# Reordering the prologues of three norms, folding squares on VectorE in the first stage, and padding two small tables

## The reference, cut to what matters

```
def rmsnorm(x, w):
    xf = x.astype(jnp.float32)
    y = xf * lax.rsqrt(jnp.mean(xf * xf, axis=-1, keepdims=True) + EPS)
    return (y * w.astype(jnp.float32)).astype(x.dtype)
def modulate(h, shift, scale):
    return h * (1 + scale) + shift
...
        h = modulate(rmsnorm(x, norm1_w[l]), sh1, sc1)
        hc = modulate(rmsnorm(ctx, norm1_w[l]), csh1, csc1)
        ...
        x = x + g2 * peer(modulate(rmsnorm(x, norm2_w[l]), sh2, sc2), w_pq[l], ...)
    return rmsnorm(x, final_norm_w)
...
def layer_ab(x, norm_g, w_in, ...):
    h = rms_norm(x, norm_g)
...
def layer_c(x, norm_g, w_in, ...):
    h = rms_norm(x, norm_g)
    u, gate = jnp.split(h @ w_in, 2, axis=-1)
```

## Time and profile before

| | |
|---|---|
| median of 3 runs (lowest, highest) | 3998.22 us (3995.88, 3999.73) |
| the profiled execution, its own time | 4002.12 us |
| its span in the trace, mean granted clock | 4000.3 us, 0.91 |
| PE busy | 3238.5 us, 81% |
| DVE busy | 2427.1 us, 61% |
| ACT busy | 1187.9 us, 30% |
| POOL busy | 929.5 us, 23% |
| HBM read | 938.51 MB |

### The profile page before, as it was taken

The page is one execution under the profiler, slowest core; times in us unless marked ns, Lnnn a source line. Parts: engine busy times, 40 slices in busy tenths (PEclk is TensorE's granted clock), DMA queues, the critical chain, the costliest instruction groups (busy, mean ns, idle before and its releaser), DMA issues. The chain is left out here.

```text
span 4000.3 us, 39602 instructions
## 1 busy us (share of the span) xinstructions
PE 3238.5 (81%) x14024; PEld 2234.9 (56%) x14024; DVE 2427.1 (61%) x3283; ACT 1187.9 (30%) x1887; POOL 929.5 (23%) x791
## 2 busy tenths in 40 slices
PE   5899998759998928777777877777998778987598
PEld 1588776538797813223322323335886667876587
DVE  1556554658776485566556655546555457869575
ACT  1432122335434401111111111103454244644553
POOL 0000010010000056544554554530001116400010
PEclk8899998869998969999999999998999579998699
DMA  9567322019864479999999999994663034530064
GB/s 355 183 213 285 122 90 85 2 47 360 313 200 147 139 298 422 422 422 422 422 422 422 422 422 422 422 422 132 185 190 116 4 117 145 173 94 4 20 192 146
DMA packets 177323, 941.98 MB, mean 235 GB/s; under 512 B 21528, under 2 KB 26776, under 8 KB 99000
## 3 DMA queue, kind: packets, MB, share of 16 engines
q0 software_dynamic: 82944, 604.02, 36.8%
q1 hardware_dynamic: 94272, 336.67, 25.5%
HBM read 938.51 MB, written 2.10 MB: 235 GB/s over the span
## 5 line engine op out<-in xcount | busy, mean ns | idle before, releaser
L1616 PE MATMUL bank<-pe_v_rows,pe_diag 128*128 128x512 f32 x1920 | 907.3, 621 | 354.5 <-DMA pe_v_rows<-in_expert_v,pe_staged_v 211.6
L1479 DVE SCALAR_TENSOR_TENSOR pe_junk<-pe_u_rows,h_rows 128x2048 f32<-128x2048 f32 x256 | 587.0, 2293 | 459.4 <-DMA pe_u_rows<-in_expert_u,pe_staged_u 448.3
L1616 PEld LDWEIGHTS bank<-pe_v_rows,pe_diag 128*128 128x128 f32 x1920 | 362.2, 197 | 899.0 <-issue 483.6
L1424 POOL DMA_INDIRECT pe_v_rows<-in_expert_v,pe_staged_v x248 | 307.9, 1242 | 359.9 <-PE bank L1616 304.6
L1424 POOL DMA_INDIRECT pe_u_rows<-in_expert_u,pe_staged_u x256 | 335.7, 1311 | 228.3 <-DVE pe_junk L1479 134.4
L1577 ACT ACTIVATE pe_diag<-ident,pe_weights 128x128 f32<-128x128 f32 x240 | 91.6, 399 | 747.5 <-PE bank L1616 747.3
L268 PE MATMUL bank<-h_parts,b_top 128*128 128x512 f32 x768 | 271.3, 399 | 9.2 <-DVE b_rest L369 9.2
L369 DVE TENSOR_TENSOR in_rest<-in_ring,in_top 128x1024 fp32r<-128x1024 f32 x112 | 138.3, 1236 | 221.1 <-ACT in_top L338 221.0
L369 DVE TENSOR_TENSOR c_rest<-c_ring,c_top 128x1024 fp32r<-128x1024 f32 x128 | 176.4, 1385 | 100.5 <-ACT c_top L338 100.2
L369 DVE TENSOR_TENSOR ab_rest<-ab_ring,ab_top 128x1024 fp32r<-128x1024 f32 x112 | 136.9, 1225 | 148.7 <-ACT ab_top L338 148.6
L270 PE MATMUL bank<-h_parts,b_rest 128*128 128x256 f32 x768 | 215.3, 280 | 0.0
(11 more groups left out here) (541 smaller groups left out, 6442.9 us busy)
## 6 DMA issues: line engine op xcount, KB each, us to landing
b_ring<-in_w_mix SPq DMA_DIRECT2D x128, 512.0 KB, 6.3
in_ring<-in_w_in SPq DMA_DIRECT2D x112, 512.0 KB, 3.7
ab_ring<-in_w_ab SPq DMA_DIRECT2D x112, 512.0 KB, 3.8
mod_ring<-in_w_mod SPq DMA_DIRECT2D x32, 1024.0 KB, 8.1
v_rows<-in_w_mod POOLq DMA_DIRECT2D x32, 1024.0 KB, 5.4
k_cols<-in_w_mod POOLq DMA_DIRECT2D x32, 1024.0 KB, 8.3
c_ring<-in_w_c_in SPq DMA_DIRECT2D x64, 512.0 KB, 4.5
c_ring<-in_w_glu_out SPq DMA_DIRECT2D x64, 512.0 KB, 4.3
```

The costliest lines, as they stand in the source:

```text
L1424: gp.indirect_dma_start(buf[:, slot, :], None, table, bass.IndirectOffsetOnAxis(ap=staged[which][:, tile, e:e + 1], axis=0)).then_inc(sems ...
L1479: nc.vector.scalar_tensor_tensor(out=junk[:, :], in0=ub[:, s, :], scalar=1.0, in1=h2tm[:, tile, :], op0=ALU.mult, op1=ALU.mult, accum_out= ...
L1616: mm = nc.tensor.matmul(banks[4 * tile + b][:, :], diag[:, e % 4, :], vb[:, s, b * 512:(b + 1) * 512], start=False, stop=False, skip_group ...
```

## The change

1. In `SplitFirst.act_start` ScalarE casts the second weight half of a norm's stream behind the first quarter of the activations, not ahead of it.
2. In `SplitFirst.dve_start` VectorE scales a quarter ahead. With a shift (`pq`) the scaling of quarter `q + 1` stands ahead of the remainder of quarter `q`; without one (`ab`, `c`) only quarters 2 and 3 are scaled together ahead of the remainders 2 and 3.
3. In `stream` TensorE's part of the norm (`hooks.pe_start`) stands ahead of its wait for the small transfers (`small_in`). Only `ab` has both.
4. In the first stage VectorE adds the 16 tiles of squares into one (five instructions), and TensorE sums that one tile with one matmul behind unit 16.
5. `gains` and `modc` are allocated with 512 bytes per partition; what is read and written in them stays the same.

```diff
--- before.py
+++ after.py
@@ -179,20 +179,36 @@
         if self.norm:
             self.norm.act_root(act)
             cast()
-            cast()
         for q in range(4):
             if self.norm:
                 self.norm.act_shift(act, q)
             self.operand.cast(act, q)
+            if self.norm and q == 0:
+                cast()
 
     def dve_start(self, dve, subtract):
         if self.norm:
+            scale, remainder = self.norm.dve_scale, self.operand.subtract
             self.norm.dve_root(dve)
-            for q in range(4):
-                self.norm.dve_scale(dve, q)
-                if q < 2:
-                    subtract()
-                self.operand.subtract(dve, q)
+            scale(dve, 0)
+            if self.norm.shift is not None:
+                scale(dve, 1)
+                subtract()
+                remainder(dve, 0)
+                scale(dve, 2)
+                subtract()
+                remainder(dve, 1)
+                scale(dve, 3)
+            else:
+                subtract()
+                remainder(dve, 0)
+                scale(dve, 1)
+                subtract()
+                remainder(dve, 1)
+                scale(dve, 2)
+                scale(dve, 3)
+            remainder(dve, 2)
+            remainder(dve, 3)
             return
         for q in range(3):
             self.operand.subtract(dve, q)
@@ -236,9 +252,9 @@
 
         @block.tensor
         def _(pe):
+            hooks.pe_start(pe)
             if small:
                 pe.wait_ge(small_in, 16 * len(small))
-            hooks.pe_start(pe)
             before = None
             for seg in segments:
                 u0, ready, free = seg["at"], seg.get("ready"), seg["free"]
@@ -417,7 +433,7 @@
         small_in, x_in = sem("mod_small_in"), sem("mod_x_in")
         unit_in = [sem(f"mod_unit_in{s}") for s in range(RING)]
         units_used, wide_zeroed = sem("mod_units_used"), sem("mod_wide_zeroed")
-        squared, summed = sem("mod_squared"), sem("mod_summed")
+        squared, summed, folded = sem("mod_squared"), sem("mod_summed"), sem("mod_folded")
         silu_done, rows_done, turned = sem("mod_silu_done"), sem("mod_rows_done"), sem("mod_turned")
         mean_done, root_done, chain = sem("mod_mean_done"), sem("mod_root_done"), sem("mod_chain")
 
@@ -467,12 +483,9 @@
                     mm = nc.tensor.matmul(banks[g][32 * b:32 * b + 32, :], c_wide[:, k, :], ring[:, u % RING, b * 512:(b + 1) * 512],
                                           start=(k == 0), stop=(k == KT - 1))
                 mm.then_inc(units_used, 1)
-                if 8 <= u < 12:
-                    pe.wait_ge(squared, u - 7)
-                    for j in range(4 * (u - 8), 4 * (u - 8) + 4):
-                        mm = nc.tensor.matmul(banks[4][:, :], con["ones"], squares[:, j, :], start=(j == 0), stop=(j == KT - 1))
-                    if u == 11:
-                        mm.then_inc(summed, 1)
+                if u == 16:
+                    pe.wait_ge(folded, 1)
+                    nc.tensor.matmul(banks[4][:, :], con["ones"], squares[:, 0, :], start=True, stop=True).then_inc(summed, 1)
 
             for g in range(2):
                 pe.wait_ge(rows_done, g + 1)
@@ -495,6 +508,11 @@
             nc.vector.tensor_copy(fast(wg_parts[0][:, :, :]), wg[:, :, :]).then_inc(split_done, 1)
             dve.wait_ge(split_done, 1)
             nc.vector.tensor_tensor(fast(wg_parts[1][:, :, :]), wg[:, :, :], wg_parts[0][:, :, :], ALU.subtract).then_inc(split_done, 1)
+            for q in range(1, 4):
+                dve.wait_ge(squared, q + 1)
+                link(nc.vector.tensor_tensor(squares[:, 0:4, :], squares[:, 0:4, :], squares[:, 4 * q:4 * q + 4, :], ALU.add))
+            link(nc.vector.tensor_tensor(squares[:, 0:2, :], squares[:, 0:2, :], squares[:, 2:4, :], ALU.add))
+            nc.vector.tensor_tensor(squares[:, 0, :], squares[:, 0, :], squares[:, 1, :], ALU.add).then_inc(folded, 1)
             dve.wait_ge(summed, 1)
             nc.vector.tensor_scalar(rstd[:, :], banks[4][:, :], 1.0 / D, EPS, ALU.mult, ALU.add).then_inc(mean_done, 1)
             dve.wait_ge(root_done, 1)
@@ -2733,7 +2751,7 @@
 def consts(nc, st, ctx, t):
     ident = ctx.enter_context(nc.sbuf_tensor("ident", [P, P], F32))
     ones = ctx.enter_context(nc.sbuf_tensor("ones", [P, P], F32))
-    gains = ctx.enter_context(nc.sbuf_tensor("gains", [P, 6, KT], F32))
+    gains = ctx.enter_context(nc.sbuf_tensor("gains", [P, 8, KT], F32))
     with st.stage() as (block, sem):
         const_in = sem("const_in")
 
@@ -2741,7 +2759,7 @@
         def _(sp):
             sp.dma_start(ident[:, :], t["c_ident"]).then_inc(const_in, 16)
             sp.dma_start(ones[:, :], t["c_ones"]).then_inc(const_in, 16)
-            sp.dma_start(gains[:, :, :], t["gains"]).then_inc(const_in, 16)
+            sp.dma_start(gains[:, 0:6, :], t["gains"]).then_inc(const_in, 16)
             sp.wait_ge(const_in, 48)
     return {"ident": ident[:, :], "ones": ones[:, :], "gains": gains}
 
@@ -2846,7 +2864,7 @@
         att = ExitStack()
         with ExitStack() as s1:
             hT = sb("hT", [P, KT, 512], s1)
-            modc = sb("modc", [P, 32, 2], s1)
+            modc = sb("modc", [P, 64, 2], s1)[:, 0:32, :]
             ring = sb("mod_ring", [P, 4, UNIT], s1)
 
             first_gates_and_modulation(st, nc, t, hT, h, ring, banks, modc, c_silu, gate_rows, con)
```

## The result

The change runs in 3953.23 us (median of 4 runs, 3943.43 to 3957.92) where the kernel before runs in 3998.97 (4 runs, 3995.88 to 4001.78). The ratio is 0.9881, 95% interval 0.9861 to 0.9901: 45.7 us less, where I had forecast 22.6 less and a range that ended at 3966. The profiled execution took 3952.45 us (4002.12 before).

The account below looks back on a forecast made before the run. Each stage has its own bound: TensorE in the streams, DMA in the expert layer, `mod_ring` in the first stage, engine handoffs in prologues. Gains 6.1 + 8.7 + 2.6 + 2.1 + 3.1 = 22.6 us gave a median of 3975.6, range 3966 to 3985.

Parts of the forecast that it names:

- the two tables: Padding `gains` and `modc` shifts every buffer behind them: costed at 0, with 34 us either way in the expert layer as bounds.
- the right rival: Aligned rows speed the gathers in the DMA-bound expert layer: up to 34 us more gained, 3942 us; chance 7%.
- the two bounds: Expert layer: 34 us faster or slower from the buffers' new starts, 2.6% of 1298 us; left outside the range.
- First stage: Square sums folded on VectorE: unit 16 no longer waits, unit 31 comes 6.1 us earlier; range 4.7 to 7.5.
- The 1.4 us around unit 24: First stage: a further 1.4 us lost with no square sums beside it, assumed to stay.
- Prologue of `pq`: Scaling a quarter ahead and the later weight cast start TensorE's last piece 8.7 us earlier; range 8 to 10.5.
- TensorE's part: Prologue of `ab`: weighted sums start without waiting for the last small table, gaining 2.6 us; range 1.3 to 3.1.
- VectorE's part: Prologue of `ab`: scalings 2 and 3 run together, so TensorE takes quarter 3 earlier, gaining 2.1 us.
- Prologue of `c`: Remainder 0 loses its 1.00 us wait and the last piece starts earlier, gaining 3.1 us; range 2 to 4.
- The first stage keeps its time: Rival: another transfer, not the square sums, starved unit 16; only the prologues' 16.5 us gained, 3981.7 us; chance 7%.
- the clock takes it back: Rival: TensorE's lower clock level lasts one unit longer in three streams, 16.8 us lost, 3992.4 us; chance 7%.
- aligned rows slow the gathers: Rival: expert layer's `pe_u_rows` and `pe_v_rows` loads lose 34 us on one common boundary, 4009.6 us; chance 4%.

Follow-up runs that it names:

- the first experiment: Two kernels: the kernel before with only `gains` and `modc` padded, 3976.52 us; the change without those two paddings, 3973.02 us.

## Why the prediction was wrong, point by point

**The step that failed** is the one on the two tables: "I cost it at nothing: the weight ring that starts at a multiple of 256 bytes has a median of 3.7 us to landing, one that starts 192 bytes past has 3.8, and the streams have TensorE in front of the DMA." The runs showed in its place 14.0 us in the expert layer (1184.5 to 1170.5; 17.0 between the padded and the unpadded kernel of the first experiment), and some 2.6 us in the first stage (unit 31 at 99.92 with, at 102.53 without padding, all else equal). With these 16.6 us the sum is 22.6 + 16.6 = 39.2 of the 45.7, and the forecast would have been 3959.0, 1.1 above the slowest run.

I had the right rival, with the right sign and in the right place, and gave it 7%. What misled me was the row that I measured it by. After the change these medians are:

```profile
in_ring<-in_w_in SPq DMA_DIRECT2D x112, 512.0 KB, 4.2
ab_ring<-in_w_ab SPq DMA_DIRECT2D x112, 512.0 KB, 4.5
```

The 128 bytes that `gains` grew by put the gathered rows on the boundary, but counted in the same way they take `in_ring` off it (128 past a multiple of 256) and leave `ab_ring` off it (64 past, 192 before). Both medians rose, and yet they can't be read as a price for that. In the 13 kernels of this case in which `in_ring` starts on the boundary its median is 3.7 to 4.3 us, and in the three in which it starts 128 past one it is 4.2, 3.8 and 3.9. The difference of 0.1 us from which I worked out 2.6% and 34 us is a sixth of that scatter. That 14.0 lies inside 34 is luck. The medians of the gathers themselves come from the stretch that DMA bounds, and there the sign shows: 33.8 us before and 33.2 after. The row that could have told was such a one, or one of throughput with DMA share at 1.00, and in the trace of the kernel before there was no second start to compare it with; I should have kept the two bounds in the range in place of leaving them outside.

The Trainium skill, page "DMA: Bandwidth & Descriptors", section "How a descriptor splits into AXI transactions", has the boundary of 256 bytes and the sign right, and my estimate from it, 1.5% or 19 us, came closer than the row that I preferred (1.2% measured, 14.0 of 1184.5). Its picture of extra beats per descriptor alone does not give the 427 GB/s with half of the rows off the boundary. Nor does it give the same cost at every distance: for a row of 8192 bytes an estimate from its beats is 258, 260 and 262 for a start 64, 128 and 192 bytes past, and the three cost the same here. Its words are of bytes that are fetched, while what moved here is where the rows are written.

**First stage, 6.1 forecast.** Right. The fold alone brought unit 31 forward by 6.8 us, inside 4.7 to 7.5. The rest of the 9.0 in the change is 1.2 us of an earlier unit 0, which the padding alone shows as well (23.5), and the faster pace. The 1.4 us around unit 24 that I left where it was came off in part. With the fold a lapse of the same kind stands earlier, 1.0 us between units 11 and 12 of the change (50.12 to 53.58) and 0.6 in the fold alone. I did not find what it is.

**Prologue of `pq`, 8.7 forecast, 8 to 10.5.** Right: 24.87 - 16.73 = 8.1 us up to the last piece, and 9.8 in the change up to the stream's end. From the reciprocal to that end it took 112.6 to 114.1 us in the three kernels with the old order and 102.3 to 104.5 in the thirteen with the new one. The granted clock behind it went from 0.98 to 1.00, which fits the 1.8 us that I had kept for the range; but kernels that all had 1.00 behind the prologue still differ by 2 us.

**Prologue of `ab`.** TensorE's part: 2.6 forecast, 3.3 measured from ScalarE's squares to the roots (2722.71 to 2735.69 before, 2682.23 to 2691.95 after), a little over the 3.1 of its range, because the 32 records then took 8.71 us in place of 9.39. VectorE's part: 2.1 forecast, 2.0 measured, from the roots to the last piece (2735.69 to 2755.26 before, 2691.95 to 2709.53 after).

**Prologue of `c`, 3.1 forecast, 2 to 4.** Too much. From the start of the reciprocal to the last piece it took 19.15 us before and 17.59 after, 1.6 less. Remainder 0 came 0.8 earlier, near the 1.0 forecast. What the replay had wrong is the piece ahead of the last: I took its four pairs at the 1.4 us of `ab`, and they took 2.7, its matmuls at 0.63 us each in place of 0.40, TensorE's lower level. In the kernel with `u` alone on the boundary the same piece ran at 0.40, and the whole took 16.4, 2.8 less than before. At the end of the first product nothing of this can be told: from the reciprocal to there it took 203.3 us before and 199.1 after, but 200.8 to 203.3 in the three kernels with the old order and 198.4 to 203.2 in the thirteen with the new one.

**The other rivals.** "The first stage keeps its time" and "the clock takes it back" did not come, "aligned rows slow the gathers" had the wrong sign.

**What stays open.** The corrected sum gives 39.2 of 45.7 us. Of the rest, 2.8 us lie between the first casts of `in` and `b`, where no instruction was edited (751.4 us before, 748.6 after). That is inside the scatter: over all 16 kernels it took 741.7 to 753.8 us, and the three with `gains` padded lie in the middle, at 748.6 to 751.1. So these 2.8 us belong to no edit that the runs could show. Why the cost of unaligned rows hides until more than half of them are unaligned is open.

## What to carry to other kernels

Where a stretch has a DMA share near 1.00, look at where its destination buffers start: one table of 384 bytes ahead of them shifted every gather by 128 bytes, and 128 more bytes of padding gave 14 us of 1184. The same padding moved `in_ring` off the boundary; no loss can be seen from it, for TensorE is in front of the DMA there (busy 567 of the 600 us from 150 to 750, with a DMA share of 0.42). So count the start of each buffer that a DMA-bound stretch fills: one padding does not align them all. Judge such an edit by the GB/s of that stretch, never by landing times in a stretch where DMA has slack. And in a prologue where two engines hand quarters to each other, let each work one quarter ahead: one order on VectorE gave 7 us of 25, and with ScalarE's cast moved too it was 8, without one instruction less.

## What the runs showed of the hardware

Where DMA is the bound, the start of a gathered row of 8192 bytes in SBUF matters to throughput by about 1.2% (427 and 422 GB/s), from a boundary of 256 bytes; the distance off it (64, 128, 192) doesn't matter, and 512 is no better. With half of the rows on the boundary the full 427 is there; with a quarter 425, with an eighth 423. At the full rate nearly every packet takes 309 ns, whichever of the two kinds of row it fills; with no row on the boundary the mean is 313.6 to 313.8. The rate acts as if two limits lay close together, of which the unaligned rows reach the second only when they are most of the traffic; that is a picture that fits five points, and nothing here shows the mechanism.
